# Adding the masked scores of both directions before they meet the values

## The chip, the cores and the metric

The kernel runs on one core of a Trainium2 chip. The metric is the device time of one execution in microseconds (us). Three runs of the kernel before took 2631.14, 2631.64 and 2631.83 us; the median is 2631.64 us. Matrix products run on TensorE (rows PE, and PEld for the loads of its stationary operand), elementwise work on VectorE (DVE) and ScalarE (ACT).

## The reference

The program is two blocks of two layers each. The change lies in the second layer of the first block, a gated linear recurrence with 16 heads of width 128 that is run forwards and backwards over 256 tokens in chunks of 64. Cut to what matters:

```python
def hgrn2_chunk_scan(q, k, v, logf, s0):
    qc, kc, vc = _chunks(q), _chunks(k), _chunks(v)
    bc = jnp.cumsum(_chunks(logf), axis=2)
    s_fin, starts = chunk_state_scan(kc, vc, bc, s0, True)
    q_dec = qc * jnp.exp(bc)
    k_inv = kc * jnp.exp(-bc)
    inter = jnp.einsum('bnchk,bnhkv->bnchv', q_dec, starts)
    scores = jnp.einsum('bnchk,bnshk->bnhcs', q_dec, k_inv)
    scores = jnp.where(mask, scores, 0.0)
    intra = jnp.einsum('bnhcs,bnshv->bnchv', scores, vc)
    return inter + intra, s_fin

# hgrn2_mixer: one scan forwards, one backwards (on flipped inputs), then
y_l = hgrn2_readout(outs_l[0] + outs_l[1], g_l, onorm_g, w_out)
```

Both directions use the same values, and only the sum of their outputs is read. So intra_f + intra_b is (scores_f + scores_b) times the values.

## The kernel before, in words

The projections of a head are split products: each fp32 weight is cut into a high part `wh` (ScalarE, `hi`, L638) and a low part `wl` (VectorE, `lo`, L1968), and `three` (L1203 to L1205, or L1206 to L1208 with the operands' roles exchanged) makes three matmuls of each pair. Weights come in chunks; the recurrence layer has eight chunks a head, each with two halves, and the buffers `wh` and `wl` hold two chunks. TensorE may start half t of chunk c when VectorE has cut its low part: `head_proj` waits for `s_lo` in front of the first product of each half.

Each engine's order is written out by hand. Heads 2 to 15 are 14 turns of a loop whose counter h sits in a register; in it `head(h)` also finishes head h - 1. Head 1 stands before the loop, head 16 and the rest of head 16's readout behind it.

- TensorE, `head(h)`: chunk 0; `head_sum(h-1)` (L1604 to L1620); `v_turn(h)` (four transposes, L1576); chunk 1; chunks 2 and 3 with `head_turn(h-1)` (L1625) and `k_turn(h, 0)` (L1586); chunk 4 and `state_scores(h, 0)` (L1596, L1601); chunk 5 and `k_turn(h, 1)`; chunks 6 and 7; `state_scores(h, 1)`.
- VectorE, `head(h)`: the low parts of chunk 0; `states(h-1, 1)` (L2552, six steps L2559, and `copy_predicated`, L2565, which writes the masked scores to `SC[:, 1]`); the first steps of `gates(0)` (L2522, L2523 and the reciprocal L2524); and only then the low parts of chunk 1. The rest of the head follows: `decay_sums`, `keys`, the moves of the turned keys (L2546), the low parts of chunks 2 to 7 between them, `states(h, 0)`.
- ScalarE, `head(h)`: moves and exponentials of the projections, `square_head(h-1)` (L930) behind `head_sum(h-1)`, the values' move (L908), logarithms and exponentials, and the high parts of the chunks.

`head_sum` computes pO (128 x 256, in PSUM) from 8 products of masked scores and values (L1612: 2 directions x 2 token tiles x 2 chunks) and 8 of decayed queries and starting states (L1617). In the profile each of these fp32 products is two records. `square_head` squares pO with a sum per row; its full result goes to the scratch `RH` in SBUF and is not read. `pQ`, the other half of pO's bank, takes the transposed head (L1625) later.

In head 16 the chunks on TensorE are those of the output projection (`out1_chunk`). They also need the finished heads cut into high and low parts (`high_y`, L764; `low_y`, L2325). There VectorE does `states(15, 1)`, L2522 to L2524, the low parts of output chunk 1 and then `low_y` for heads 5 to 8, for which TensorE's next product waits. After head 16 come `states(16, 1)`, then `head_sum(16)`.

Of the kernel before, what the change touches and what calls it, by code (L numbers as in the profile page):

```python
# [10 lines left out]
ACT = mybir.ActivationFunctionType  # L11
ALU = mybir.AluOpType
AX = mybir.AxisListType

P = 128
D = 2048
KT = D // P
SEQ = 256
TOK = 2 * SEQ
EPS = 1e-6  # L20
CHUNK = 64
# [224 lines left out]
def first_block_and_hybrid(nc, a):  # L246

    ctx = ExitStack()
    with ctx:
# [3 lines left out]
        def sem(name):  # L253
            return ctx.enter_context(nc.semaphore(name))
# [19 lines left out]
        def C(name, n=None):  # L274
            w = dict(CONSTS)[name] if n is None else n
            return cst[:, CCOL[name]:CCOL[name] + w]
# [4 lines left out]
        def area(at, *dims):  # L281
            n = int(np.prod(dims))
            v = arena[:, at:at + n]
            if len(dims) == 2:
                v = v.rearrange("p (a b) -> p a b", a=dims[0])
            if len(dims) == 3:
                v = v.rearrange("p (a b c) -> p a b c", a=dims[0], b=dims[1])
            return v
# [29 lines left out]
        W1b = W1 + 8 * TOK  # L318
        Q, SG, GH = (area(W1b + SEQ * i, SEQ) for i in range(3))
        IT, V1, KD = area(W1b + 768, TOK), area(W1b + 1280, 4, P), area(W1b + 1792, 4, P)  # L320
        ST = area(W1b + 2304, 2, 4 * P)
        SX = area(W1b + 3328, 2, P)
        SC = area(W1b + 3584, 2, 2 * P)
        OS, RH = area(W1b + 4096, SEQ), area(W1b + 4352, SEQ)
        DEC = small[:, 360:376].rearrange("p (d n) -> p d n", d=2)
        GB1 = area(W1b + 4608, 1, D)
        XR1 = area(2 * W1, 2, D // 2)
        pT, pO, pQ = ps[:, 4, :], ps[:, 7, 0:SEQ], ps[:, 7, SEQ:TOK]
# [28 lines left out]
        oss, ors, LN = small[:, 312:314], small[:, 314:316], small[:, 332:334]  # L357
# [79 lines left out]
        s_hev = sem("head_moved")  # L437
        s_f, s_ln, s_b, s_ex, s_kdr = sem("forget_ready"), sem("log_forget"), sem("decay_summed"), sem("decay_exp"), sem("keys_ready")
        s_vT, s_v, s_kT, s_kd = sem("v_turned"), sem("v_ready"), sem("k_turned"), sem("k_moved")
        s_ds, s_st, s_scp, s_sc = sem("state_steps"), sem("states_ready"), sem("scores"), sem("scores_masked")  # L440
        s_o, s_rso, s_oT, s_y1 = sem("head_summed"), sem("head_scaled"), sem("head_turned"), sem("head_out")
        s_sgr = sem("head_gate")
        s_l1, s_l1m = sem("layer1_region_free"), sem("layer1_modulation")
# [184 lines left out]
        def _(act):  # L628
            step = Chain(act, s_act)
# [12 lines left out]
            for t, rows in enumerate(PARAM_ROWS):  # L642
                at = 0
# [230 lines left out]
            def head(h, split, comp=True, fin=True, moved=None, between=None, final=False):  # L874
# [29 lines left out]
                if fin:  # L904
                    square_head(h - 1)
# [21 lines left out]
            def square_head(h):  # L927
                act.wait_ge(s_o, 2 * h)
                for t in range(2):
                    step(nc.scalar.activation(RH[:, t * P:(t + 1) * P], pO[:, t * P:(t + 1) * P], ACT.Square, accum_out=oss[:, t:t + 1]))  # L930

            def head_rms(h):
                step.done()
# [42 lines left out]
            hi(st.chunk("out1", 1, 0), halves=(0,))  # L976
            step(nc.scalar.activation(small[:, 506:507], eps, ACT.Ln)).done()
            square_head(HEADS)
            head_rms(HEADS)
            x_rows = lambda t: x_save[t * P:(t + 1) * P, :]  # L980
# [218 lines left out]
        def _(pe):  # L1199
# [402 lines left out]
                ins.then_inc(s_scp, 1)  # L1602

            def head_sum(h):  # L1604
                pe.wait_ge(s_sc, h * 2 + 2)
                pe.wait_ge(s_st, h * 2 + 1)
                pe.wait_ge(s_y1, h)
                for d in range(2):
                    for t in range(2):
                        for c in range(2):  # L1610
                            at = t * P + c * CHUNK
                            nc.tensor.matmul(pO[c * CHUNK:(c + 1) * CHUNK, t * P:(t + 1) * P], SC[:, d, at:at + CHUNK], V1[:, t, :],  # L1612
                                             start=(d == 0 and t == 0), stop=False, skip_group_check=True)
                for d in range(2):
                    for n in range(4):
                        t, c = n // 2, n % 2
                        ins = nc.tensor.matmul(pO[c * CHUNK:(c + 1) * CHUNK, t * P:(t + 1) * P], QD[:, d, n * CHUNK:(n + 1) * CHUNK],  # L1617
                                               ST[:, d, n * P:(n + 1) * P], start=False, stop=(d == 1 and t == 1), skip_group_check=True)
                        if d == 1 and t == 1:
                            ins.then_inc(s_o, 1)  # L1620
# [7 lines left out]
            def head(h, chunk, comp=True, fin=True, turn_at=3):  # L1628

                for c in range(8):  # L1630
                    chunk(c)
                    if fin and c == 0:
                        head_sum(h - 1)
                    if comp and c == 0:
                        v_turn(h)
                    if fin and c == turn_at:
                        head_turn(h - 1)
                    if comp and c == 3:
                        k_turn(h, 0)
                    if comp and c == 4:  # L1640
                        state_scores(h, 0)
                    if comp and c == 5:
                        k_turn(h, 1)
                    if comp and c == 7:
                        state_scores(h, 1)
# [51 lines left out]
            head(HEADS, out_before, turn_at=2)  # L1697
            out1_chunk(7, (0, 1), True)
            head_sum(HEADS)
            out1_chunk(6, (2,))  # L1700
            out1_chunk(7, (2,), True)
# [258 lines left out]
        def _(dve):  # L1960
            step = Chain(dve, s_dve)
# [552 lines left out]
            def head(h, split, comp=True, fin=True, between=None, final=False):  # L2514
# [33 lines left out]
                def states(h, d):  # L2548

                    dve.wait_ge(s_ds, h * 2 - 1 + d)  # L2550
                    at = lambda n: ps[:, 5 + n % 2, (n // 2) * P:(n // 2 + 1) * P]
                    step(nc.vector.tensor_copy(SX[:, 0, :], at(ORDER[d][0]))).done()  # L2552
                    src = SX[:, 0, :]
                    for j in range(1, 7):
                        n = ORDER[d][j]
                        if j == 6:
                            dve.wait_ge(s_scp, h * 2 - 1 + d)
                        dst = SX[:, j % 2, :] if j < 3 else ST[:, d, ORDER[d][j + 1] * P:(ORDER[d][j + 1] + 1) * P]
                        ins = nc.vector.scalar_tensor_tensor(out=dst, in0=src, scalar=DEC[:, d, n:n + 1], in1=at(n),  # L2559
                                                             op0=ALU.mult, op1=ALU.add)  # L2560
                        if j < 6:
                            step(ins).done()
                        src = dst
                    ins.then_inc(s_st, 1)
                    nc.vector.copy_predicated(SC[:, d, :].rearrange("p (a b) -> p a b", a=2),  # L2565
                                              C(("mask_f", "mask_b")[d]).bitcast(I32).unsqueeze(1).broadcast_to([P, 2, P]),
                                              pT[:, 0:SEQ].rearrange("p (a b) -> p a b", a=2)).then_inc(s_sc, 1)

                def head_out(h):

                    dve.wait_ge(s_oT, h)
                    y = Y1[:, bass.ds(h - 1, 1), :].rearrange("p a b -> p (a b)")
                    nc.vector.tensor_tensor(y, pQ, y, ALU.mult).then_inc(s_y1, 1)
# [13 lines left out]
                if fin:  # L2587
                    states(h - 1, 1)
# [17 lines left out]
                else:  # L2606
# [8 lines left out]
                    split(5)  # L2615
                    silu(h)
                states(h, 0)
                split(6)
                k_move(1)
                split(7)  # L2620

            def head_chunks(h):
                return lambda c: lo(st.chunk("hg", h, c), 10 * P)

            head(1, head_chunks(1), fin=False, between=angles)
            with dve.Fori(2, HEADS) as h, step.loop(h, 2, HEADS - 2, 24):
                head(h, head_chunks(h))


            def out_chunks(c):  # L2630
                if c < 7:
                    lo(st.chunk("out1", 0, c))
                for k in {0: range(4), 1: range(4, 8), 2: range(8, 12), 4: range(12, 14), 5: (14,)}.get(c, ()):
                    low_y(k, Y1[:, k, :], SEQ, KT)

            head(HEADS, out_chunks, final=True)
            head(HEADS + 1, lambda c: lo(st.chunk("out1", c, 7 * (1 - c)), halves=(0,) if c else (0, 1)), comp=False)
            low_y(KT - 1, Y1[:, KT - 1, :], SEQ, KT)
# [341 lines left out]
```

## Time and profile before

| | |
|---|---|
| median of three runs | 2631.64 us |
| the profiled execution | 2631.77 us |
| its span | 2630.0 us |
| TensorE busy (rows PE) | 2575.5 us, 98% of the span |
| VectorE busy | 1824.1 us, 69% |
| ScalarE busy | 1174.0 us, 45% |
| mean granted TensorE clock | 0.996 |

The profile is one execution. The busy time of an engine is an average over many stages; which engine sets the time at a given place has to be read from the timeline there. A row of the timeline merges equal instructions that follow each other: it gives their first start, the time from it to the last end, and their number. Where two instructions of an engine overlap in the rows, the later one was started while the earlier one was still draining.

### The profile page before, as it was taken

How to read it: one execution, taken by the hardware profiler on the slowest of the kernel's cores; microseconds unless marked ns; L12 is line 12 of the kernel's file. 1: busy time of each engine (PE TensorE's matmuls, PEld its weight loads, DVE VectorE, ACT ScalarE, POOL GpSimd, SP SyncE). 2: the span in 40 equal slices, each digit the busy share in tenths (PEclk: the TensorE clock that was granted, in tenths of full speed). 3: DMA queues.
4: the chain of work that ended last, by engine and by line, in shares of the span. 5: the costliest groups of instructions: out<-in, count | busy, mean ns of one | idle time of the engine just before them, and what ended most of it. 6: DMA issues, size and time to landing. Idle time of an engine off the chain costs nothing.

```text
span 2630.0 us, 36547 instructions
## 1 busy us (share of the span) xinstructions
PE 2575.5 (98%) x13669; PEld 2126.4 (81%) x13669; DVE 1824.1 (69%) x2625; ACT 1174.0 (45%) x1988; POOL 0.2 (0%) x4
## 2 busy tenths in 40 slices
PE   5999999999999999999999999999999999999998
PEld 2678788888788888888888888778888887978887
DVE  2369788788886677776777677866566656656674
ACT  3422121223225644544454454556455646555563
POOL 0000000000000000000000000000000000000000
PEclk8999999999999999999999999999999999999999
DMA  9975466565664333333333333465544465644464
GB/s 371 374 261 161 144 192 213 166 205 185 217 208 151 93 109 90 109 100 110 93 106 105 94 110 106 156 216 177 165 149 151 160 229 188 183 144 156 149 211 142
DMA packets 404684, 437.14 MB, mean 166 GB/s; under 512 B 22735, under 2 KB 286681, under 8 KB 403033
## 3 DMA queue, kind: packets, MB, share of 16 engines
q1 hardware_dynamic: 396864, 414.24, 49.2%
q10 hardware_dynamic: 7704, 21.34, 2.2%
q8 instruction: 75, 1.23, 0.2%
q14 instruction: 41, 0.33, 0.0%
HBM read 427.14 MB, written 8.39 MB: 166 GB/s over the span
## 4 chain that ended last, share of the span: by engine, by line
PE 91%; DVE 4%; ACT 2%; DMA 2%; issue 1%; ACTq 0%; DVEq 0%; SPq 0%
PE ps L1203 16%; PE ps L1204 16%; PE ps L1205 16%; PE ps L1206 11%; PE ps L1208 11%; PE ps L1207 11%; DVE wl L1968 1%; DMA raw<-in_ada_w_dram 1%; PE ps L1596 1%; PE ps L1227 1%; PE ps L1900 1%; PE ps L1601 1%; PE ps L1886 1%; PE ps L1612 1%; ACT hTh L1004 1%
## 5 line engine op out<-in xcount | busy, mean ns | idle before, releaser
L1968 DVE TENSOR_TENSOR wl<-raw,wh 128x1024 fp32r<-128x1024 f32 (+1 forms) x682 | 701.8, 1058 | 368.6 <-ACT wh L638 359.2
L638 ACT ACTIVATE wh<-raw 128x1024 fp32r<-128x1024 f32 (+1 forms) x682 | 614.5, 929 | 750.8 <-PE ps L1205 413.8
L1203 PE MATMUL ps<-hTh,wh 128*128 128x512 f32 (+1 forms) x2076 | 757.0, 365 | 3.3 <-DVE wl L1968 2.0
L1204 PE MATMUL ps<-hTl,wh 128*128 128x512 f32 (+1 forms) x2076 | 747.1, 360 | 0.0
L1205 PE MATMUL ps<-hTh,wl 128*128 128x512 f32 (+1 forms) x2076 | 745.9, 359 | 0.0
L1206 PE MATMUL ps<-wh,hTh 128*128 128x512 f32 (+1 forms) x1440 | 572.3, 397 | 8.5 <-DVE wl L1968 4.0
L1208 PE MATMUL ps<-wh,hTl 128*128 128x512 f32 (+1 forms) x1440 | 556.2, 386 | 0.0
L1207 PE MATMUL ps<-wl,hTh 128*128 128x512 f32 (+1 forms) x1440 | 554.7, 385 | 0.0
L1203 PEld LDWEIGHTS ps<-hTh,wh 128*128 128x128 f32 x2076 | 392.5, 189 | 69.1 <-issue 5.8
L1204 PEld LDWEIGHTS ps<-hTl,wh 128*128 128x128 f32 x2076 | 392.5, 189 | 59.3 <-issue 1.2
L1205 PEld LDWEIGHTS ps<-hTh,wl 128*128 128x128 f32 x2076 | 391.6, 189 | 60.1
L1206 PEld LDWEIGHTS ps<-wh,hTh 128*128 128x128 f32 x1440 | 270.8, 188 | 66.9 <-DVE wl L1968 9.9
L1208 PEld LDWEIGHTS ps<-wh,hTl 128*128 128x128 f32 x1440 | 270.5, 188 | 54.9
L1207 PEld LDWEIGHTS ps<-wl,hTh 128*128 128x128 f32 x1440 | 271.2, 188 | 50.8 <-issue 1.9
L2031 DVE SCALAR_TENSOR_TENSOR acc<-raw,small,acc 128x1024 f32<-128x1024 f32 x180 | 217.5, 1280 | 0.0
L2524 DVE RECIPROCAL arena<-arena 128x512 f32<-128x512 f32 x32 | 107.1, 3347 | 0.0
L1104 ACT ACTIVATE arena<-arena,small 128x256 f32<-128x256 f32 (+1 forms) x112 | 49.6, 444 | 124.2 <-DVE small L2822 69.4
L2559 DVE SCALAR_TENSOR_TENSOR arena<-arena,small,ps 128x128 f32<-128x128 f32 x192 | 66.8, 348 | 6.8
L1227 PE MATMUL ps<-raw,s 128*32 128x512 f32 x320 | 45.9, 679 | 15.4 <-DMA raw<-in_ada_w_dram 13.3
L2552 DVE COPY arena<-ps 128x128 f32<-128x128 f32 x32 | 9.2, 288 | 73.8 <-PE ps L1596 73.8
L881 ACT ACTIVATE arena<-ps 128x512 f32<-128x512 f32 x32 | 17.4, 595 | 74.2 <-PE ps L1205 74.2
L930 ACT ACTIVATE arena<-ps 128x128 f32<-128x128 f32 x32 | 8.6, 273 | 84.4 <-PE ps L1617 84.4
(310 smaller groups left out, 2079.3 us busy)
## 6 DMA issues: line engine op xcount, KB each, us to landing
raw<-in_ada_w_dram SPq DMA_DIRECT2D x96, 1024.0 KB, 6.3
raw<-in_w_in_dram SPq DMA_DIRECT2D x88, 1024.0 KB, 5.1
raw<-in_od_w_in_dram SPq DMA_DIRECT2D x256, 320.0 KB, 3.5
raw<-in_ev_w_in_dram SPq DMA_DIRECT2D x192, 256.0 KB, 4.3
raw<-in_w_out_dram SPq DMA_DIRECT2D x32, 1024.0 KB, 5.1
raw<-in_ev_w_out_dram SPq DMA_DIRECT2D x16, 1024.0 KB, 5.1
raw<-in_od_w_out_dram SPq DMA_DIRECT2D x16, 1024.0 KB, 5.2
arena<-x_save ACTq DMA_DIRECT2D x12, 512.0 KB, 9.2
```

The lines of the kernel that those rows point to most:

```text
L638: nc.scalar.activation(wh[:, ch.spl, part], raw[:, ch.raw, part], ACT.Copy).then_inc(s_hi, 1)
L1203: nc.tensor.matmul(out, w_h, x_h, start=first, stop=False, skip_group_check=True)
L1204: nc.tensor.matmul(out, w_h, x_l, start=False, stop=False, skip_group_check=True)
L1205: return nc.tensor.matmul(out, w_l, x_h, start=False, stop=last, skip_group_check=True)
L1206: nc.tensor.matmul(out, x_h, w_h, start=first, stop=False, skip_group_check=True)
L1207: nc.tensor.matmul(out, x_h, w_l, start=False, stop=False, skip_group_check=True)
L1208: return nc.tensor.matmul(out, x_l, w_h, start=False, stop=last, skip_group_check=True)
L1227: ins = nc.tensor.matmul(psA(n)[32 * t:32 * (t + 1), :], s2[:, 2 * k:2 * k + 32], raw[:, ch.raw, t * BLK:(t + 1) * BLK], start=(c == 0), s ...
L1968: nc.vector.tensor_tensor(wl[:, ch.spl, part], raw[:, ch.raw, part], wh[:, ch.spl, part].bitcast(F32), ALU.subtract).then_inc(s_lo, 1)
L2031: ins = nc.vector.scalar_tensor_tensor(out=acc[:, v, :], in0=w, scalar=silc[:, k:k + 1], in1=acc[:, v, :], op0=ALU.mult, op1=ALU.add)
L2524: step(nc.vector.reciprocal(R[:, d, :], R[:, d, :])).done()
L2559: ins = nc.vector.scalar_tensor_tensor(out=dst, in0=src, scalar=DEC[:, d, n:n + 1], in1=at(n), op0=ALU.mult, op1=ALU.add)
```

## The change

```diff
-        OS, RH = area(W1b + 4096, SEQ), area(W1b + 4352, SEQ)
+        OS, SS = area(W1b + 4096, SEQ), area(W1b + 4352, SEQ)
...
-        s_ds, s_st, s_scp, s_sc = ...
+        s_ds, s_st, s_scp, s_sc, s_ss = ..., sem("scores_summed")
...
             def square_head(h):
                 act.wait_ge(s_o, 2 * h)
                 for t in range(2):
-                    step(nc.scalar.activation(RH[:, t * P:(t + 1) * P], pO[...], ACT.Square, accum_out=oss[:, t:t + 1]))
+                    step(nc.scalar.activation(pQ[:, t * P:(t + 1) * P], pO[...], ACT.Square, accum_out=oss[:, t:t + 1]))
...
             def head_sum(h):
-                pe.wait_ge(s_sc, h * 2 + 2)
+                pe.wait_ge(s_ss, h)
                 pe.wait_ge(s_st, h * 2 + 1)
                 pe.wait_ge(s_y1, h)
-                for d in range(2):
-                    for t in range(2):
-                        for c in range(2):
-                            at = t * P + c * CHUNK
-                            nc.tensor.matmul(pO[...], SC[:, d, at:at + CHUNK], V1[:, t, :],
-                                             start=(d == 0 and t == 0), stop=False, skip_group_check=True)
+                for t in range(2):
+                    for c in range(2):
+                        at = t * P + c * CHUNK
+                        nc.tensor.matmul(pO[...], SS[:, at:at + CHUNK], V1[:, t, :],
+                                         start=(t == 0), stop=False, skip_group_check=True)
...
                     nc.vector.copy_predicated(SC[:, d, :]..., mask, pT[:, 0:SEQ]...).then_inc(s_sc, 1)
+                    if d:
+                        dve.wait_ge(s_sc, h * 2 + 2)
+                        nc.vector.tensor_tensor(SS, SC[:, 0, :], SC[:, 1, :], ALU.add).then_inc(s_ss, 1)
```

Per head, four of the eight products of scores and values are gone (8 of 16 records). VectorE adds the two masked score tiles (128 x 256 fp32, all in SBUF) at the end of `states(h, 1)`, after a wait for its own `copy_predicated`, and TensorE waits for that sum. The scratch of `square_head` moves from SBUF to pQ in PSUM, because the sum takes its place.

## Rows read from the trace of the kernel before

**Rows 1.** Stretch of the recurrence loop: span, busy us of PE, PEld, DVE, ACT, POOL.
```profile
944.40:1665.80 721.40, 721.40 (x4503) 625.70 (x4502) 539.35 (x817) 344.83 (x638) 0.00 (x0) 1.00 0.35 105
```

**Rows 2.** Timeline (start, us, instruction): first, one middle and last head sum in the loop.
```profile
944.44 1.09 PE L1612 MATMUL ps<-arena 128*64 128x128 f32 x16
...
1099.04 1.09 PE L1612 MATMUL ps<-arena 128*64 128x128 f32 x16
1099.96 1.04 PE L1617 MATMUL ps<-arena 128*64 128x128 f32 x16
...
1101.32 0.19 PEld L1203 LDWEIGHTS ps<-hTh,wh 128*128 128x128 f32 x1
...
1614.37 1.09 PE L1612 MATMUL ps<-arena 128*64 128x128 f32 x16
```

**Rows 3.** Timeline, VectorE over the same turn's start.
```profile
1092.94 0.29 DVE L2552 COPY arena<-ps 128x128 f32<-128x128 f32 x1 [5.04 <-PE ps L1596]
...
1095.45 0.44 DVE L2565 COPY_PREDICATED arena<-cst,ps 128x256 f32<-128x256 int32 x1
...
1095.78 0.42 DVE L2522 TENSOR_SCALAR arena<-arena 128x512 f32<-128x512 f32 x1
...
1096.37 0.49 DVE L2523 TENSOR_SCALAR arena<-arena,small 128x512 f32<-128x512 f32 x1 [0.17 <-DVE arena L2522]
...
1096.77 3.35 DVE L2524 RECIPROCAL arena<-arena 128x512 f32<-128x512 f32 x1
...
1100.24 0.83 DVE L1968 TENSOR_TENSOR wl<-raw,wh 128x640 fp32r<-128x640 f32 x1
```

**Rows 4.** Timeline, VectorE in the loop: instructions without and with a wait between them.
```profile
1064.37 0.42 DVE L2541 TENSOR_TENSOR arena<-arena 128x256 f32<-128x256 f32 x1
1064.70 0.42 DVE L2542 TENSOR_TENSOR arena<-arena 128x256 f32<-128x256 f32 x1
...
1073.22 0.29 DVE L2578 TENSOR_SCALAR arena<-arena 128x256 f32<-128x256 f32 x1
1073.54 1.75 DVE L2579 RECIPROCAL arena<-arena 128x256 f32<-128x256 f32 x1
```

**Rows 5.** Timeline, TensorE released by VectorE after the loop.
```profile
1720.55 1.23 DVE L1968 TENSOR_TENSOR wl<-raw,wh 128x1024 fp32r<-128x1024 f32 x1 [2.85 <-ACT wh L638]
...
1721.83 0.19 PEld L1206 LDWEIGHTS ps<-wh,hTh 128*128 128x128 f32 x1 [1.47 <-DVE wl L1968]
```

**Rows 6.** Timeline, first loads of low parts and last needs of the head before.
```profile
1053.30 1.56 DVE L1968 TENSOR_TENSOR wl<-raw,wh 128x640 fp32r<-128x640 f32 x2 [1.71 <-ACT wh L638]
...
1055.34 0.19 PEld L1203 LDWEIGHTS ps<-hTh,wh 128*128 128x128 f32 x1
...
1071.15 0.69 DVE L2546 COPY arena<-ps 128x512 f32<-128x512 f32 x1
...
1072.87 0.96 PEld L1596 LDWEIGHTS ps<-arena 64*128 64x128 f32 x14
```

**Rows 7.** Timeline, head 16 behind the loop.
```profile
1662.32 0.45 DVE L2565 COPY_PREDICATED arena<-cst,ps 128x256 f32<-128x256 int32 x1
...
1669.16 1.43 DVE L2325 TENSOR_TENSOR hTl<-arena,hTh 128x256 fp32r<-128x256 f32 x4
...
1669.70 0.19 PEld L1206 LDWEIGHTS ps<-wh,hTh 128*128 128x128 f32 x1 [1.55 <-DVE wl L1968]
```

**Rows 8.** Timeline, the last head sum.
```profile
1709.04 0.44 DVE L2565 COPY_PREDICATED arena<-cst,ps 128x256 f32<-128x256 int32 x1
...
1709.84 0.85 PEld L1612 LDWEIGHTS ps<-arena 128*64 128x64 f32 x16 [0.35 <-DVE arena L2565]
...
1717.76 0.19 PEld L1206 LDWEIGHTS ps<-wh,hTh 128*128 128x128 f32 x1 [0.46 <-DVE hTl L2325]
```

**Rows 9.** Timeline, ScalarE behind a head sum in the loop.
```profile
1101.08 0.28 ACT L930 ACTIVATE arena<-ps 128x128 f32<-128x128 f32 x1 [5.49 <-PE ps L1617]
...
1101.63 0.60 ACT L908 ACTIVATE arena<-ps 128x512 f32<-128x512 f32 x1
```

More of the change, by code:

```diff
@@ L439, in first_block_and_hybrid @@
         s_vT, s_v, s_kT, s_kd = sem("v_turned"), sem("v_ready"), sem("k_turned"), sem("k_moved")
-        s_ds, s_st, s_scp, s_sc = sem("state_steps"), sem("states_ready"), sem("scores"), sem("scores_masked")
+        s_ds, s_st, s_scp, s_sc, s_ss = sem("state_steps"), sem("states_ready"), sem("scores"), sem("scores_masked"), sem("scores_summed")
         s_o, s_rso, s_oT, s_y1 = sem("head_summed"), sem("head_scaled"), sem("head_turned"), sem("head_out")
@@ L929, in square_head @@
                 for t in range(2):
-                    step(nc.scalar.activation(RH[:, t * P:(t + 1) * P], pO[:, t * P:(t + 1) * P], ACT.Square, accum_out=oss[:, t:t + 1]))
+                    step(nc.scalar.activation(pQ[:, t * P:(t + 1) * P], pO[:, t * P:(t + 1) * P], ACT.Square, accum_out=oss[:, t:t + 1]))
             def head_rms(h):
@@ L1604, in head_sum @@
             def head_sum(h):
-                pe.wait_ge(s_sc, h * 2 + 2)
+                pe.wait_ge(s_ss, h)
                 pe.wait_ge(s_st, h * 2 + 1)
                 pe.wait_ge(s_y1, h)
-                for d in range(2):
-                    for t in range(2):
-                        for c in range(2):
-                            at = t * P + c * CHUNK
-                            nc.tensor.matmul(pO[c * CHUNK:(c + 1) * CHUNK, t * P:(t + 1) * P], SC[:, d, at:at + CHUNK], V1[:, t, :],
-                                             start=(d == 0 and t == 0), stop=False, skip_group_check=True)
+                for t in range(2):
+                    for c in range(2):
+                        at = t * P + c * CHUNK
+                        nc.tensor.matmul(pO[c * CHUNK:(c + 1) * CHUNK, t * P:(t + 1) * P], SS[:, at:at + CHUNK], V1[:, t, :],
+                                         start=(t == 0), stop=False, skip_group_check=True)
                 for d in range(2):
```

## Prediction, made before the changed kernel ran

> **What bounds the kernel now.** I read the busy times of the recurrence loop first, then its timeline, since the loop is nearly all of the only stage that the change touches; the reader is to look for the engine that is never idle there. Between 944.40 and 1665.80 us TensorE is busy for 721.40 of 721.40 us, VectorE for 539.35 [rows 1]. So in the loop TensorE sets the time, and work taken from it is worth its full length, but only if TensorE finds what it needs next. That is read from the timeline around one head sum. TensorE starts the eight score products (16 records of L1612) at 1099.04 and the eight state products at 1099.96, then four transposes, and the first product of chunk 1 loads its weights at 1101.32 [rows 2]. The other side of that moment is on VectorE. It is released by TensorE's state products at 1092.94, finishes the states, masks the scores (1095.45), does L2522, L2523 and a reciprocal of 3.35 us, and only then cuts the first half of chunk 1: 1100.24 to 1101.07 [rows 3]. TensorE may not start chunk 1 before that. After an L1968 that it waited for, TensorE loaded weights 0.05 us behind its end (1720.55 + 1.23 = 1721.78, load at 1721.83) [rows 5]. So the half was usable at 1101.12, and TensorE came at 1101.32: the margin is **0.20 us**. Head sums follow each other at (1614.37 - 944.44) / 13 = 51.53 us [rows 2], and the timelines of the 14 turns show the same offsets to within 0.02 us.
>
> **What the change removes.** 8 of 16 records of L1612 a head. The 16 take 1099.96 - 1099.04 = 0.92 us [rows 2], 0.0575 each, so TensorE is through with a head sum 0.46 us earlier. Sixteen heads would make 7.4 us. In the loop this saving lies in front of the chunk 1 that has only 0.20 us of margin; at most 0.20 could be kept even if VectorE were given nothing new.
>
> **What it adds on VectorE.** A 128 x 256 fp32 addition in SBUF behind a wait for the masking, in front of L2522. The same form, L2541, takes 0.42 us, and with no wait between them the next instruction starts 0.33 to 0.34 us after it started (1064.37, 1064.70) [rows 4]: it overlaps by 0.09. With a wait for the instruction in front, the next starts after its end: 0.03 us after in the loop (L2578 at 1073.22, 0.29 long, L2579 at 1073.54) [rows 4], but 0.12 behind L2524, where a second wait follows, and 0.17 in front of L2523, which takes an operand addressed by the loop's register [rows 3]. The new addition has fixed addresses and one wait, so I take 0.04. Today L2522 starts 0.33 us after the masking (1095.45, 1095.78) [rows 3]. After: 0.44 (masking) + 0.04 + 0.33 = 0.81. VectorE gets to everything behind it **0.48 us later** a head; bounds 0.34 (the addition at its pitch and the wait free) and 0.61 (the wait at 0.17).
>
> Where such a wait costs, the Trainium skill ("VectorE: DVE Perf Modes", section "The DRAIN you can't avoid") says that semaphores between VectorE instructions cost nothing extra and that the pipeline drains anyway. By that the delay would be the low bound. The trace disagrees: 0.33 us from start to start for a 0.42 us instruction without a wait, and a start behind the end with one [rows 4].
>
> **The sum in the loop, 14 heads (sums of heads 1 to 14).** The first half of chunk 1 is usable at 1101.12 + 0.48 = 1101.60. TensorE, at 1101.32 - 0.46 = 1100.86, waits 0.74 us and starts 0.28 later than now. The masks' sum itself is done at about 1096.4, 2.7 us before the head sum needs it, so the new wait on `s_ss` costs nothing. Behind chunk 1 VectorE is late by 0.48 - 0.28 = 0.20 relative to TensorE. The next cuts have room: chunk 2's first half is done before 1054.2 and needed at 1055.34; the turned keys are moved at 1071.84 and needed at 1072.87 [rows 6]; the chunks between are alike, 0.9 us or more. VectorE then idles 5.04 us before the next L2552 [rows 3], where it is back in step with TensorE, so nothing is carried from head to head except TensorE's 0.28: 14 x 0.28 = **+3.9 us**.
>
> **Head 16, behind the loop (sum of head 15).** TensorE already waits 1.55 us for VectorE at 1669.70, for L2325 behind the same chain [rows 7]; the 0.46 is lost in that wait and VectorE's 0.48 goes through: **+0.5 us**. **The last sum.** Masking ends at 1709.48 [rows 8]; the addition from 1709.52 to 1709.94, TensorE at 1709.99 in place of 1709.84, +0.15, and 0.46 shorter behind it: **-0.3 us**. What follows, the wait at 1717.76 [rows 8], hangs on the end of that sum and keeps it. VectorE's next cut there has over a microsecond of room.
>
> **The square's scratch.** ScalarE's squares (1101.08) and the reads of their sums are over by about 1101.7, while the values' move behind them waits for the transposes anyway and starts at 1101.63 [rows 9]. No row has ScalarE writing PSUM, so I bound it by L930's own 0.28 us either way, twice a head. In the loop TensorE releases ScalarE 0.46 us earlier while what ScalarE needs next from VectorE comes 0.48 later, so up to 0.56 us is covered there; only behind the last sum is it on the path, at most 0.56 us once, taken as 0. The Trainium skill ("ScalarE: Activation LUTs", in its note that a ScalarE result goes to PSUM faster than to SBUF) would make this a small gain; no row here shows it.
>
> **Total.** 3.9 + 0.5 - 0.3 = +4.1 us. The profiled execution took 2631.77 us, 0.13 above the median, so 2631.64 + 4.1 = **2635.7 us**, +0.16%. A measurement of this kernel can tell about 0.2%, 5.3 us, from no change; the forecast lies just inside.
>
> **The rivals.**
> 1. *The wait shows its register arithmetic* (slower). In the loop the value that the addition waits for is computed from the register; if that falls behind the masking and not beside it, the wait costs 0.17 as in front of L2523 [rows 3], and VectorE is 0.61 late. 0.61 - 0.20 = 0.41 a head, 14 x 0.41 = 5.7, with +0.5 and -0.3 behind the loop +5.9: 2637.5. It decides from a wait of 0.11 up (0.55 of delay: 14 x 0.35 + 0.2 = 5.1). For it: two rows in the loop above 0.1. Against: both have a reason that the addition lacks, and L2579, with a wait and no such reason, costs 0.03. A few hundredths of extra release time a head would lead to the same place.
> 2. *The wait is free*, as the skill's page would have it: delay 0.34, 14 x 0.14 = 2.0, +0.3, and the last sum keeps its 0.46: +1.8, 2633.5. Against it stand the starts of [rows 4].
> 3. *TensorE's saving comes through* (faster). If chunk 1 is not what TensorE meets at 1101.32, or VectorE's chain is not in front of it, then 14 x 0.46 and 0.46 for the last sum are gained: -6.9, 2624.7. For it: no wait is recorded at that product today, and the margin is inferred, not seen. Against: the order by hand puts L1968 of chunk 1 there, and the ends of the two sides keep their 0.20 us in every turn. Even with VectorE's addition free it could not gain more than 14 x 0.20 + 0.46 = 3.3.
>
> **Chances.** Forecast 0.62 (its own range 2634.5 to 2637.2), rival 1 with its kin 0.23, rival 2 0.08, rival 3 0.07. Most of the forecast and all of rival 2 lie within 0.2%, a few hundredths of the forecast above it: faster 0.07, same 0.66, slower 0.27. The range is 2632.9 to 2638.2; it takes in rivals 1 and 2 and leaves out rival 3.
>
> **What would show it.** Of the changed kernel: L1612 with 128 records in place of 256; an added VectorE row of 0.42 us behind L2565, starting 0.04 behind its end, and L2522 0.81 us behind the start of L2565; a new idle time of about 0.7 us a head on PEld or PE at L1203, released by L1968 in the loop; head sums 51.81 us apart in place of 51.53; and no longer wait at L1612. Wrong if there is no such idle time at L1203, if the turns are closer than 51.53, or if TensorE waits at another chunk.

## The result

The changed kernel takes 2636.71 us (median of 19 runs) against 2631.64 us before (median of 19): +5.07 us. The ratio to the kernel before is 1.0020, with a 95% interval of 1.0012 to 1.0027. The forecast was 2635.7 with a range of 2632.9 to 2638.2. One disturbed run of the 19, of 4871.66 us, is left out of the ratio. The profiled execution is one of the shorter runs, 2635.45 us, with a span of 2633.7 us.

The timeline of the changed kernel around one head sum shows what happens in the loop (start, duration, instruction; in brackets the idle time and what ended it). It answers to [rows 2, 3]; lines behind the diff are numbered otherwise (L1611 was L1612, L1616 was L1617, L1967 was L1968, and L2521 was L2522).

```profile
1093.78 0.29 DVE L2551 COPY arena<-ps 128x128 f32<-128x128 f32 x1 [5.04 <-PE ps L1596]
...
1096.28 0.44 DVE L2564 COPY_PREDICATED arena<-cst,ps 128x256 f32<-128x256 int32 x1
1096.76 0.43 DVE L2569 TENSOR_TENSOR arena<-arena 128x256 f32<-128x256 f32 x1
1097.10 0.42 DVE L2521 TENSOR_SCALAR arena<-arena 128x512 f32<-128x512 f32 x1
...
1101.56 1.56 DVE L1967 TENSOR_TENSOR wl<-raw,wh 128x640 fp32r<-128x640 f32 x2
```

```profile
1099.87 0.66 PE L1611 MATMUL ps<-arena 128*64 128x128 f32 x8
...
1100.36 1.04 PE L1616 MATMUL ps<-arena 128*64 128x128 f32 x16
...
1101.33 0.42 PEld L1576 LDWEIGHTS ps<-cst,arena 128*128 128x128 f32 x4 [0.17 <-issue]
...
1102.44 0.19 PEld L1203 LDWEIGHTS ps<-hTh,wh 128*128 128x128 f32 x1 [0.69 <-DVE wl L1967]
```

On VectorE the addition starts 0.04 us behind the masking's end and L2521 starts 0.82 us behind the masking's start; before it was 0.33 [rows 3]. On TensorE the eight records of L1611 give way to L1616 after 0.49 us, where the sixteen took 0.92 [rows 2]. Then comes what the kernel before did not have: 0.69 us of idle weight loading in front of the first product of chunk 1, ended by VectorE's cut of that chunk. The waits of TensorE's weight loads on VectorE's cuts, between 940 and 1650 us, count it (total, times, longest):

```profile
PEld ps L1203 <- DVE wl L1967: 9.7, 14, 0.7
```

Fourteen turns, 0.69 us each. The first and the last head sum in the loop of the changed kernel:

```profile
944.38 0.66 PE L1611 MATMUL ps<-arena 128*64 128x128 f32 x8
...
1618.20 0.66 PE L1611 MATMUL ps<-arena 128*64 128x128 f32 x8
```

They lie (1618.20 - 944.38) / 13 = 51.83 us apart; before, 51.53 [rows 2]. So each turn is 0.30 us longer, 4.2 us in 14. In head 16 the product that starts at 1669.70 before [rows 7] starts here at 1674.31, behind 2.48 us of idle time in place of 1.55. And behind the last sum the load at 1717.76 [rows 8] is here at 1722.10:

```profile
1673.78 1.42 DVE L2324 TENSOR_TENSOR hTl<-arena,hTh 128x256 fp32r<-128x256 f32 x4
...
1674.31 0.19 PEld L1206 LDWEIGHTS ps<-wh,hTh 128*128 128x128 f32 x1 [2.48 <-DVE wl L1967]
...
1722.10 0.19 PEld L1206 LDWEIGHTS ps<-wh,hTh 128*128 128x128 f32 x1 [0.47 <-DVE hTl L2324]
```

The bracket names the cut L1967, but that had ended by 1673.86; as in the kernel before, what fits the load's start is the end of the first of the four L2324 behind it. The differences to before are +4.61 and +4.34 us. The rest of the profiled execution gave 0.6 us back (the spans differ by 3.7), outside the changed stage.

### The profile page after: what moved, and what is told of

Read it like the earlier page. It is cut to its first block, busy times and chain, and to the rows that moved or that the text cites. A ratio compares the mean times of both kernels' runs of the same rounds, so it can differ in the third digit from the quotient of the medians.

```text
span 2633.7 us, 36321 instructions
## 1 busy us (share of the span) xinstructions
PE 2572.0 (98%) x13541; PEld 2117.8 (80%) x13541; DVE 1831.3 (70%) x2641; ACT 1174.1 (45%) x1988; POOL 0.2 (0%) x4
## 4 chain that ended last, share of the span: by engine, by line
PE 86%; DVE 8%; ACT 2%; DMA 2%; issue 2%; ACTq 0%; DVEq 0%; SPq 0%
PE ps L1203 15%; PE ps L1204 15%; PE ps L1205 15%; PE ps L1206 11%; PE ps L1208 11%; PE ps L1207 11%; DVE arena L2523 2%; DVE wl L1967 2%; DMA raw<-in_ada_w_dram 2%; PE ps L1596 1%; DVE arena L2558 1%; PE ps L1227 1%; PE ps L1899 1%; PE ps L1885 1%; ACT hTh L1004 1%
## 5 line engine op out<-in xcount | busy, mean ns | idle before, releaser
L1967 DVE TENSOR_TENSOR wl<-raw,wh 128x1024 fp32r<-128x1024 f32 (+1 forms) x682 | 701.5, 1057 | 364.3 <-ACT wh L638 354.9
L1227 PE MATMUL ps<-raw,s 128*32 128x512 f32 x320 | 46.0, 676 | 16.4 <-DMA raw<-in_ada_w_dram 14.0
L930 ACT ACTIVATE ps<-ps 128x128 f32<-128x128 f32 x32 | 8.5, 266 | 77.6 <-PE ps L1616 77.6
```

Source lines behind the costliest of these rows:

```text
L1227: ins = nc.tensor.matmul(psA(n)[32 * t:32 * (t + 1), :], s2[:, 2 * k:2 * k + 32], raw[:, ch.raw, t * BLK:(t + 1) * BLK], start=(c == 0), s ...
L1967: nc.vector.tensor_tensor(wl[:, ch.spl, part], raw[:, ch.raw, part], wh[:, ch.spl, part].bitcast(F32), ALU.subtract).then_inc(s_lo, 1)
```

## The experiments

Every experiment was timed in five rounds, in turns with the kernel before. Where a text says "head sums apart", it is the distance of the first and the last in the loop, over 13. The ratio goes by the kernel before as it ran in turns with each: its median was 2631.71 us beside the first four experiments, 2631.53 beside the next four and 2631.37 beside the last three (both with the high part first, and the addition in the gap). Where a gain below is given against "before" it is against 2631.64, except where the text says otherwise.

| kernel | head sums apart, us | median, us | ratio to before, 95% |
|---|---|---|---|
| before | 51.53 | 2631.64 | |
| changed | 51.83 | 2636.71 | 1.0012 to 1.0027 |
| fewer products alone | 51.34 | 2628.51 | 0.9976 to 0.9994 |
| addition alone | 51.83 | 2636.46 | 1.0008 to 1.0026 |
| before, early cut | 51.53 | 2631.63 | 0.9988 to 1.0006 |
| changed, early cut | 51.11 | 2625.69 | 0.9966 to 0.9985 |
| changed, scratch in SBUF | 51.83 | 2635.87 | 1.0006 to 1.0025 |
| changed, addition twice | 52.16 | 2640.99 | 1.0021 to 1.0049 |
| changed, early cut, addition twice | 51.11 | 2626.78 | 0.9975 to 0.9993 |
| changed, early cut in heads 1 to 15 | 51.11 | 2624.26 | 0.9962 to 0.9983 |
| changed, early cut, high part first | 51.11 | 2622.48 | 0.9956 to 0.9980 |
| changed, early cut in heads 1 to 15, high part first | 51.11 | 2623.65 | 0.9958 to 0.9982 |
| changed, addition in the gap | 51.40 | 2629.91 | 0.9985 to 1.0004 |

**The two halves of the change.** First TensorE's half by itself:

```diff
 def head_sum(h):
     pe.wait_ge(s_sc, h * 2 + 2)
-    for d in range(2): ... SC[:, d, at:at + CHUNK] ... start=(d == 0 and t == 0)
+    ... SC[:, 0, at:at + CHUNK] ... start=(t == 0)
```

> The kernel before with TensorE's half of the change alone: four products of scores and values a head in place of eight, made from the forward scores; no addition on VectorE, and the backward scores stay out of the result. Theory (chunk 1's low half, usable 0.20 us before TensorE comes for it, is what TensorE meets next): TensorE is 0.46 us early, waits 0.26 us a head at the first product of chunk 1 and keeps 0.20: 14 x 0.20 + nothing in head 16 + 0.46 in the last sum = 3.3 us faster than before, 2628.4. Rival (TensorE's saving comes through, nothing stands behind it): 14 x 0.46 + 0.46 = 6.9 us faster, 2624.7, and no idle time at L1203 in the loop.

Measured: 2628.51 us, 3.2 less than before in its own rounds. The timeline of this kernel has the small wait that the theory asks for, 14 times, with VectorE's work exactly as before:

```profile
1100.18 0.42 PEld L1576 LDWEIGHTS ps<-cst,arena 128*128 128x128 f32 x4 [0.17 <-issue]
...
1100.80 0.19 PEld L1203 LDWEIGHTS ps<-hTh,wh 128*128 128x128 f32 x1 [0.20 <-DVE wl L1967]
```

Of the 0.43 us that TensorE saves it keeps 0.20 a head and waits for the rest. So even a free addition could not have brought the saving home: the kernel before had a margin of 0.20 us there, though it recorded no wait.

Then VectorE's half:

```diff
-    ... SS[:, at:at + CHUNK] ... (four products)
+    for d in range(2): ... SC[:, d, at:at + CHUNK] ... (eight, behind the wait for the sum)
```

> The changed kernel with VectorE's half alone: it adds the scores and TensorE waits for the sum, but makes all eight products from the two masked tiles as before. Theory: in the loop TensorE's four products are worth nothing, so it stands where the changed kernel does: 14 x 0.30 + 0.5 in head 16 + 0.2 at the last sum = 4.9 us over before, 2636.5, with the idle time at L1203 some 0.2 to 0.3 us a head in place of 0.69. Rival (the changed kernel is the sum of a saving of 7.4 on TensorE and a cost elsewhere): 7.4 us above the changed kernel, 11.8 over before, 2643.5.

Measured: 2636.46 us, and head sums 51.83 us apart, the same as in the changed kernel. TensorE does twice the score products here and ends at the same time; only its wait is shorter (total, times, longest, 940 to 1650 us):

```profile
PEld ps L1203 <- DVE wl L1968: 3.6, 14, 0.3
```

The two halves are not additive: -3.2 and +4.8 us would make +1.6, and together they make +5.1. In the loop the time is the later of two arrivals, and once VectorE is late TensorE's part no longer counts.

**Giving VectorE's cut its place back.** The cut of chunk 1 is moved in front of the first gate, in the kernel before and in the changed one:

```diff
-                gates(0, lambda: split(1))
+                split(1)
+                gates(0, lambda: None)
```

> The kernel before, with VectorE's cut of chunk 1 moved from behind the reciprocal of the first gate to in front of that gate's first instruction. Theory: in the loop TensorE never waited for it, so 0 there; in head 16 TensorE's wait of 1.55 us goes: 1.3 to 1.6 us faster, 2630.2. VectorE's work up to the gate's end is the same in sum, so ScalarE's logarithm is not later. Rival (the gate's chain is what counts, and it is now 1.5 us later for the reciprocal): slower, up to 14 x 0.5 us.

> The changed kernel with the same move. Theory: chunk 1 is ready over 2 us before TensorE comes, so TensorE's 0.46 us a head comes through in the loop: 14 x 0.46 = 6.4; in head 16 the wait of 1.55 us and 0.46 go, 2.0; the last sum keeps 0.3: 8.7 us faster than before, 2622.9, no idle time at L1203 in the loop. Rival (the added work or the new wait costs TensorE time in another place than chunk 1, or the PSUM scratch does): it stays near the changed kernel, above 2631.

In the loop both came out as the theory has it: head sums 51.53 us apart in the first, as before, and 51.11 in the second. There TensorE goes from the transposes to chunk 1 with no idle time:

```profile
1608.88 0.42 PEld L1576 LDWEIGHTS ps<-cst,arena 128*128 128x128 f32 x4 [0.17 <-issue]
1609.27 0.19 PEld L1203 LDWEIGHTS ps<-hTh,wh 128*128 128x128 f32 x1
```

The difference, 0.43 us a head, is the full worth of four products, now on the path: 6.0 us in 14 heads. The medians, 2631.63 and 2625.69 us, are both above what was expected, 2630.2 and 2622.9. The expectation for head 16 was wrong: I took TensorE's wait of 1.55 us away and thought the time went with it. The timeline of head 16 in the kernel before with the early cut says where it went:

```profile
1674.62 0.19 PEld L1206 LDWEIGHTS ps<-wh,hTh 128*128 128x128 f32 x1 [2.79 <-DVE wl L1968]
...
1675.42 0.25 PEld L1207 LDWEIGHTS ps<-wl,hTh 128*128 128x128 f32 x1
1675.77 0.33 PEld L1208 LDWEIGHTS ps<-wh,hTl 128*128 128x128 f32 x1
1676.20 0.33 PEld L1206 LDWEIGHTS ps<-wh,hTh 128*128 128x128 f32 x1
1676.62 0.33 PEld L1207 LDWEIGHTS ps<-wl,hTh 128*128 128x128 f32 x1
```

Head 16 is bound by VectorE over two chunks; the waits of 1.55 and 1.20 us at chunks 1 and 2 became one of 2.79 at chunk 2. And from 1675.42 on the products of 512 columns follow each other after 0.43 us in place of 0.23: TensorE ran at its lower clock of 1.2 GHz. The stretches of that kernel (window, length, busy us of PE, PEld, DVE, ACT, POOL, then granted clock, DMA share, GB/s) show the granted clock fall:

```profile
1670.00:1674.00 4.00, 2.24 (x10) 1.51 (x9) 2.35 (x3) 3.81 (x8) 0.00 (x0) 1.00 0.00 0
1674.00:1677.00 3.00, 2.35 (x7) 1.92 (x8) 2.97 (x7) 2.98 (x4) 0.00 (x0) 0.75 0.46 133
1677.00:1680.00 3.00, 3.00 (x11) 2.36 (x10) 3.00 (x4) 2.96 (x9) 0.00 (x0) 0.68 0.58 222
```

What the fall costs can be read off. From the load at 1674.62 to the last head sum this kernel takes 34.98 us, and the kernel before takes 33.61 from the same load. First the last head sum here, then the load in the kernel before:

```profile
1709.60 0.85 PEld L1612 LDWEIGHTS ps<-arena 128*64 128x64 f32 x16 [0.35 <-DVE arena L2565]
```

```profile
1676.23 0.19 PEld L1206 LDWEIGHTS ps<-wh,hTh 128*128 128x128 f32 x1 [1.20 <-DVE wl L1968]
```

The sums are 1709.60 - 1674.62 here and 1709.84 [rows 8] - 1676.23 before; the difference is 1.37 us. From the sum of head 15 to the last one this kernel takes 45.39 us (1664.21 to 1709.60) and the kernel before 44.01 (1665.83 to 1709.84). Take the 1.37 away and they are the same: the early cut by itself changes nothing in head 16.

The eleven runs of the kernel before with the early cut fall into two groups: four at 2630.11 to 2630.46 us, where I had put them, with a mean granted clock of 0.996, and seven at 2631.59 to 2632.26, six of which have 0.994 or 0.995. The profile is of the second group, and the distance of the two, 1.5 us, is about the price of one fall; that the first group is the runs without a fall is likely, but no profile shows one of them. The mean clock alone doesn't tell it: it also holds the low clock of the first 50 us, and the kernel with fewer products has 0.994 in its profile with a clock of 1.00 in head 16.

What the early cut does gain outside the loop is in head 1, which stands before it: there TensorE waited 1.67 us for the same cut, and no longer does; behind it TensorE is 1.4 us ahead. That gain is what put the first group at 2630.2, and not the one that I expected in head 16.

**One long wait or two.** To see what the clock has to do with it, head 16 got its old order back:

```diff
+                if not final:
+                    split(1)
+                gates(0, (lambda: split(1)) if final else (lambda: None))
```

> The changed kernel with chunk 1 cut early in heads 1 to 15 alone; head 16 as in the changed kernel. In the kernel with the early cut in all heads TensorE's two waits in head 16 (2.48 and 1.20 us in the changed kernel) became one of 3.72 us, and the granted clock was 0.74 and 0.83 in the 8 us around its end. Theory (that drop costs 1.2 to 1.6 us and comes from the one long idle stretch): two waits again, granted clock 1.00 in head 16, head sums 51.11 apart, about 2624.3, 1.4 below the kernel with the early cut everywhere. Rival (the drop comes in any order, or head 16's time is VectorE's alone and the clock costs nothing): no difference to 2625.7.

Measured: 2624.26 us, 1.43 below the early cut in all heads, as expected. But the reason is not quite the expected one. The wait in front of chunk 1, which ends at 1662.64, is 2.48 us again, and in this profile the clock fell at its end too:

```profile
1660.00:1665.00 5.00, 2.73 (x10) 2.04 (x9) 4.68 (x8) 2.57 (x7) 0.00 (x0) 0.75 0.26 83
1665.00:1670.00 5.00, 5.00 (x22) 4.07 (x21) 3.64 (x7) 4.54 (x9) 0.00 (x0) 0.91 0.36 133
```

Here the slower products lie in front of the second wait of 1.20 us for VectorE, which is no longer seen: the slow clock used up time that TensorE would have waited. In the kernel with one wait nothing behind it took the loss up. From the sum of head 15 to the last one the profiles show 45.16 us here (1658.29 to 1703.45) and 46.03 with the early cut everywhere (1658.46 to 1704.49), so this accounts for 0.87 of the 1.43 us; where the rest comes from is open, and the clock itself can't be held fixed.

**What the PSUM scratch does.**

```diff
-        OS, SS = area(W1b + 4096, SEQ), area(W1b + 4352, SEQ)
+        OS, RH = area(W1b + 4096, SEQ), area(W1b + 4352, SEQ)
+        SS = area(W1b + 1792, SEQ)
...
-  activation(pQ[...], pO[...], ACT.Square, ...)
+  activation(RH[...], pO[...], ACT.Square, ...)
```

> The changed kernel with the square's unread result in SBUF again; the scores' sum lies in the turned keys' buffer, which is free then. Theory (the scratch is hidden in the loop): head sums 51.83 us apart as in the changed kernel, the last sum's chain at most 0.1 us longer, 2636.5 to 2636.8 by the median. Rival (the PSUM scratch is part of the loss, or saves time that hides a larger one): over 1 us away from the changed kernel, and another distance of the head sums.

Measured: 2635.87 us and the same distance of the head sums, 51.83. The median is below the expected 2636.5 and 0.8 us below the changed kernel's, but the intervals of the two ratios overlap over nearly their whole length, so this study can't tell them apart. The profiles of the two show something more useful. Both have the wait of 2.48 us in head 16, in the same place, and the next stretch is at full clock in the changed kernel's profile and not in this one's. First the changed kernel, then the one with the scratch in SBUF:

```profile
1675.00:1680.00 5.00, 5.00 (x23) 3.82 (x21) 3.32 (x5) 3.58 (x7) 0.00 (x0) 1.00 0.60 209
```

```profile
1675.00:1680.00 5.00, 5.00 (x16) 3.95 (x15) 3.32 (x5) 3.70 (x8) 0.00 (x0) 0.66 0.59 205
```

So behind the same wait the clock falls in some executions and not in others. From that load to the last head sum the changed kernel takes 40.27 us (1674.31 to 1714.58), this one 40.87 (1674.19 to 1715.06): in the order with a second wait of 1.20 us a fall costs 0.6 us and not 1.4. The square itself takes 266 ns into PSUM in the changed kernel and 274 into SBUF before (medians), which shows nowhere in these times.

**A dose on VectorE.** The addition is done twice, the first time into a buffer that is not read; once in the changed kernel, once with the early cut:

```diff
+    nc.vector.tensor_tensor(KD[:, 0:2, :]..., SC[:, 0, :], SC[:, 1, :], ALU.add)
     nc.vector.tensor_tensor(SS, SC[:, 0, :], SC[:, 1, :], ALU.add).then_inc(s_ss, 1)
```

> The changed kernel with the addition done twice, the first time into a buffer that is not read. Theory (each microsecond that VectorE is later in front of chunk 1 is one on the time): 0.34 us more a head, head sums 52.17 us apart, 14 x 0.34 + 0.34 in head 16 + 0.34 at the last sum = 5.4 us over the changed kernel, 2642.1. Rival (the loss is the wait for the masking or the semaphore to TensorE, not VectorE's time): under 1 us more.

> The same double addition in the kernel that cuts chunk 1 ahead of the first gate. Theory: in the loop it is hidden, head sums stay 51.11 us apart as in that kernel; head 16 is bound by VectorE and the last sum waits for the addition, 0.34 each: 0.7 us over that kernel's 2625.7, 2626.4. Rival (VectorE's time in the loop is on the path wherever it stands): 5 us over it, 2630.7.

Measured: 2640.99 us (five runs, spread over 2.9 us) with head sums 52.16 apart, and 2626.78 with 51.11. The same 0.34 us on VectorE costs 0.33 us a head in the one order and nothing a head in the other. The medians fit less closely: 4.3 us where 5.4 was expected, and 1.1 where 0.7 was. In the profile of the first, the changed stage adds 5.2 us, as expected (the whole execution is 2.06 us late before the loop, where the clock fell at 66 us, at the end of a wait of 3.09); in the profile of the second the clock fell in head 16 for twice as long as in the others. That is the plainest statement of the case: what an addition costs is decided by what stands behind it.

**The addition in a gap.** L2522 of the changed kernel waits for L2521 in any case, and VectorE idles 0.17 us there in the loop:

```diff
 step(nc.vector.tensor_scalar(R, Z, 1e30, 1.0, ALU.min, ALU.add))
+if d == 0 and fin:
+    dve.wait_ge(s_sc, ...); tensor_tensor(SS, SC[:, 0, :], SC[:, 1, :], ALU.add)
 step.done()
 step(nc.vector.tensor_scalar(Z, Z, 1e30, bound(oml, d), ALU.min, ALU.mult))
```

> The changed kernel with the addition moved behind L2522, in front of L2523, where VectorE idles 0.17 us for L2522 anyway; no early cut. Theory: from L2522's start to L2523's 0.59 us become 0.68 or so, VectorE is 0.1 us late in place of 0.50, inside the margin of 0.20: TensorE keeps 0.1 a head, head sums 51.43 apart, 14 x -0.1 + 0.2 in head 16 - 0.3 at the last sum = 1.5 below before, 2630.2. Rival (the addition costs its 0.34 to 0.5 wherever it stands): 2635 to 2636.7.

Measured: 2629.91 us, head sums 51.40 apart, 0.13 under before. The median is 1.5 us under before in its own rounds, as expected, but the interval of the ratio takes in 1, so as a gain it is not shown; that the 5 us of loss are gone is. VectorE's timeline in this kernel:

```profile
1095.13 0.44 DVE L2567 COPY_PREDICATED arena<-cst,ps 128x256 f32<-128x256 int32 x1
1095.47 0.42 DVE L2521 TENSOR_SCALAR arena<-arena 128x512 f32<-128x512 f32 x1
1095.80 0.42 DVE L2572 TENSOR_TENSOR arena<-arena 128x256 f32<-128x256 f32 x1
1096.14 0.48 DVE L2525 TENSOR_SCALAR arena<-arena,small 128x512 f32<-128x512 f32 x1
```

From the first gate instruction to the second it is 0.67 us in place of 0.59 [rows 3]: the idle 0.17 us in front of the second gate instruction is filled, and the addition no longer starts behind the masking's end but 0.33 us behind the start of the instruction in front of it. The same addition costs VectorE 0.08 us here and 0.49 behind the masking.

**Less waiting in head 16.** VectorE idles 1.65 us there for the high part of output chunk 2, which ScalarE makes behind a logarithm that waits for VectorE. ScalarE makes it first:

```diff
+                    if final:
+                        split(2)
                     log_forget(0)
-                split(2)
+                if not final:
+                    split(2)
```

> The kernel with the early cut in all heads, and in head 16 ScalarE also makes the high part of output chunk 2 before the first logarithm, so that VectorE no longer idles 1.65 us for it (1673.42 in the kernel before). Theory: head 16 is bound by VectorE, so 1.65 us less idle there is 1.65 less time, and TensorE's one wait of 3.72 us becomes about 2.1, short enough to keep the clock more often: 1.65 plus up to 1.5 below 2625.7, 2622.5 to 2624.0. Rival (ScalarE's chain is what bounds head 16): no gain or a loss.

> The same high part first, with the early cut in heads 1 to 15 alone: TensorE's waits in head 16 are 2.48 us at chunk 1 and, in place of 1.20, none at chunk 2. Theory: 1.2 us below 2624.3 where the clock holds, less where it falls behind the 2.48 us wait and no second wait is left to take up the slower products: 2623.1 to 2624.3. Rival (as above): no gain or a loss.

Measured: 2622.48 and 2623.65 us. In the profile of the first the single wait of TensorE in front of chunk 2 is down to 1.98 us and the clock holds:

```profile
1667.51 0.19 PEld L1209 LDWEIGHTS ps<-wh,hTh 128*128 128x128 f32 x1 [1.98 <-DVE wl L1970]
```

```profile
1665.00:1670.00 5.00, 3.41 (x16) 2.50 (x15) 4.96 (x8) 4.93 (x8) 0.00 (x0) 1.00 0.32 91
```

By the median it is the fastest kernel of the study, 9 us under the kernel before (ratio 0.9956 to 0.9980) and 14 under the changed one; its interval overlaps those of the two kernels with the early cut in heads 1 to 15. In the second the wait stays at 2.48 us; its runs fall into 2622.65 to 2622.97 and 2624.33 to 2624.82, and its profile, a run of the second group, shows the fall.

## Why the prediction was right, step by step

- **TensorE is not what decides at chunk 1.** Right. The margin of 0.20 us, inferred from two ends that never met in a recorded wait, was measured by the kernel with fewer products: 0.20 us kept a head.
- **The saving on TensorE.** I took 0.46 us a head, half of the time that sixteen records took. It is 0.43 (51.53 less 51.11; the eight take 0.49 us to the next group, not 0.46). In the loop of the changed kernel it plays no part either way.
- **VectorE's delay.** Predicted 0.48, measured 0.49 (0.82 less 0.33). The wait behind the masking cost 0.04 us, as taken. Rival 1, the register's arithmetic behind the masking, is refuted by that, and rival 2, the free wait, by the same row: with the wait the next instruction starts 0.48 us behind the masking's start, without one 0.33 [rows 3]. The Trainium skill ("VectorE: DVE Perf Modes", section "The DRAIN you can't avoid") says that a semaphore costs nothing extra there; here it costs 0.15 us.
- **The loop.** Predicted +0.28 a head, measured +0.30; 4.2 us in place of 3.9.
- **Head 16 and the last sum.** Predicted +0.5 and -0.3; measured 4.61 - 4.12 = +0.49 (the start of that head's states is 1663.93 in the changed profile and 1659.81 before) and 4.34 - 4.61 = -0.27.
- **Sum.** The trace gives +4.3 at the end of the changed stage where +4.1 was forecast, and the medians +5.07. The 0.7 us between them are not explained, and the measurement can't tell them from nothing: the interval of the ratio, 1.0012 to 1.0027, is +3.2 to +7.1 us. What the prediction did not have is that the clock can fall. TensorE's wait in head 16 grew from 1.55 to 2.48 us, and behind such a wait it fell in other kernels. In the changed kernel no profile caught it, and it could not give the whole: in the same order, with the scratch in SBUF, a fall cost 0.6 us, and that kernel, whose profile has it, stands +4.3 us over before in its own rounds. The prediction also took 5.3 us as the least that a measurement tells from no change; the interval is 3.9 us wide and clear of 1.
- **The PSUM scratch** was taken as 0, and nothing speaks against it: the kernel without it has the same head sums and a median within the noise.

## What to carry to other kernels

Before work is taken off the busiest engine, read what it meets next and how early that is ready: a wait that is not recorded may be 0.20 us away, and beyond it the saving buys idle time. Work moved to another engine costs what stands behind it there; here 0.34 us of addition cost 0.33 a head or nothing, by the place of one cut of a weight chunk, and the move of that cut turned a loss of 5 us into a gain of 6. Where an engine is bound by another over a long stretch, taking one wait away only lengthens the next one.

## What the runs showed of the hardware

The granted clock after idle stretches of TensorE was not expected. The table has the longest wait in head 16 of each profile (one execution each) and how long the granted clock behind it stood at 0.50, that is at 1.2 GHz in place of 2.4. The means under 1.00 in the stretches above come from where the stretch lies, not from a third level: cut into single microseconds, they are 1.00 and 0.50, apart from those that hold an edge.

| kernel | longest wait, us | at 1.2 GHz |
|---|---|---|
| before | 1.55 | not at all |
| changed, early cut, high part first | 1.98 | not at all |
| fewer products alone | 1.99 | not at all |
| addition alone | 2.04 | not at all |
| addition in the gap | 2.19 | some 3 us |
| changed | 2.48 | not at all |
| scratch in SBUF | 2.48 | some 3 us |
| early cut in heads 1 to 15 | 2.48 | some 3 us |
| early cut in heads 1 to 15, high part first | 2.48 | some 3 us |
| before, early cut | 2.79 | some 3 us |
| addition twice | 2.81 | not at all |
| changed, early cut | 3.72 | some 3 us |
| changed, early cut, addition twice | 4.06 | some 7 us |

In the first four the clock held; in seven of the other nine it fell, and equal waits of 2.48 us came out both ways. Nor is the length of a wait enough by itself: in all 13 profiles TensorE also waits 2.3 to 2.7 us at 89 to 92 us (L1227 in the kernel before), and the clock held there each time. That the wait is the cause was not tested; for it speaks that between 100 and 2600 us the clock fell in no profile anywhere but at this wait. What a fall costs is in the products behind it, 0.43 us from one to the next in place of 0.23: 1.37 us in the kernel before with the early cut, and 0.6 where a later wait takes part of it up. The other surprise is small: the addition on VectorE cost 0.08 us in the gap between two dependent instructions, and 0.49 behind the wait for the masking.
